# A two-block network on one core: bias products behind the fourth unit, and modulation rows on four column tiles

## The chip, the cores and the metric

One core of one Trainium2 chip runs one program, in float32. The metric is the device time of an execution in microseconds; lower is better.

## The reference

The reference computes two blocks on a sequence of 512 tokens of width 1024. The first has an input projection, native sparse attention with a bias by distance, a convolution branch, gated linear attention (GLA), a gated FFN and a per-layer embedding gate (PLE). The second has a modulated norm over 512 tokens and 256 context tokens, a Fourier branch, an RWKV branch and a convolutional FFN. Two parts of it matter here. One is the bias row of the attention, a table of 32 buckets by 8 heads read by distance and masked:

```python
def head_bias(dist):
    return bias_h[:, t5_bucket(dist)].reshape(Hk, G, *dist.shape)
```

The other is the modulation: six vectors of 1024 for the tokens (`c`) and six for the context (`c_ctx`), 6144 numbers each:

```python
mod_x = jax.nn.silu(c) @ ada_w[l] + ada_b[l]
sh1, sc1, g1, sh2, sc2, g2 = [m[:, None, :] for m in jnp.split(mod_x, 6, axis=-1)]
h = modulate(rms_norm_2(x, norm1_g[l]), sh1, sc1)
```

The weights of the modulation, 1024 x 6144, do not depend on the first block, so their products can be done anywhere before the second.

## The kernel before, in words

All arrays lie in one SBUF tensor and are transposed: 128 channels on the partitions, tokens in the free dimension. Weights come as **units** of 128 x 8 x 128 floats (512 KB), in one fixed order (`STREAM`), through a ring of four slots. SyncE loads the ring (L2368, L2372): four units at the start, then unit n + 4 into the slot of unit n as soon as TensorE's products on unit n are done (`units_done`). In the common use of a unit (`product`, L331) eight products of 128x128 by 512 columns are summed in a PSUM bank; one takes two matmul records in the trace.

Each engine runs its own list, stage by stage, and semaphores tie them. The order on each engine is written out by hand.

**Start** (`start`, then `norm1`). ScalarE's queue issues four tiles of x, the constants (identity and ones), the columns of small parameters, and three small arrays for the bias (`onehot`, `rel_bias`, `negmask`). All five arrays after x count on one semaphore, `ld_start`. TensorE waits for all five, multiplies the bias table with the one-hot array (L450, two products of 8 x 320), and then sums the squares of `norm1` with a matrix of ones (L399). ScalarE makes the squares (L369), then the logarithm and exponential of the root (L373, L374), VectorE scales the tiles (L407), and the 17 units of the input projection follow (`project1`, L331). VectorE adds the mask to the bias row (L461), and ScalarE later stores it to DRAM and reads it back as tiles.

**Modulation rows** (`ada_units`, L905). The weights are 48 units, four for each of twelve blocks `b` of 512 columns. Of unit q of a block, two products have the pair of activated vectors (`cs`, two columns) as weights and 512 columns of the unit as the moving operand; eight such products are summed in a bank of 2 x 512. ScalarE copies the two rows to `modrow` (`ada_row`, L921). When six blocks are there, 24 small transposes bring each piece of 2 x 128 to 128 x 2 (`ada_turn`, L915), and VectorE adds the bias column (`ada_columns`, L926).

Where these units stand:

- blocks 0 to 5 in the GLA stage: four units first, with the sum of the context's squares behind them (L895); one unit in each of the eight chunks of the recurrence, between the product with the state (L1021) and the update of the state (L1027, which VectorE's L1063 and L1064 follow); then four units, a sum of squares (L1034), eight units, the turn;
- block 6 behind the sum of the norm ahead of the first FFN, block 7 behind that of the norm ahead of the PLE gate: they cover the time in which ScalarE and VectorE make the root and the first scaled tile;
- block 8 ahead of the sum of the last norm of the first block (L393, L395), which waits for POOL's additions (L385);
- blocks 9 to 11 right behind that sum, then the sum of the second block's norm (L399) and the second turn.

For the steps of the prediction: L735 are transposes of 128x128 in the attention, L672 the narrow products of the compression MLP (weights 128x64, two column tiles), L1812 the wide products of the RWKV recurrence (64x64 tiles, 128 columns, four positions in turn), L1053 VectorE's multiply that makes the scaled key of the GLA, L961 the exponential it needs.

## Time and profile before

| | us |
|---|---|
| median of 3 runs | 2170.36 (2165.15 to 2174.89) |
| profiled execution, its own time | 2162.62 |
| profiled execution, span of the trace | 2160.4 |
| TensorE matmul busy | 2006.7 (93%) |
| VectorE busy | 759.6 (35%) |
| ScalarE busy | 483.2 (22%) |
| POOL busy | 193.7 (9%) |
| mean granted TensorE clock | 0.958 of full |

The span is from the first to the last instruction. Busy times of engines overlap. The weight loads of TensorE are listed by themselves (PEld) and run beside its matmuls. In 2160 us the DMA engines move 157.73 MB, 73 GB/s on the mean.

### The profile page before, as it was taken

The numbers are of one execution on the slowest core, as the hardware profiler recorded it, in microseconds if no ns is written. First come the engines' busy times: TensorE is split into PE (matmuls) and PEld (weight loads), VectorE is DVE, ScalarE is ACT, GpSimd is POOL, SyncE is SP. The second block draws the span as 40 slices with busy tenths as digits, with TensorE's granted clock in tenths as the row PEclk, the third lists the DMA queues.
The fourth block names the chain that finished last, engine by engine and source line by source line (L and its number), as shares of the span: only waits on it lengthen the run. The fifth ranks groups of instructions, "written<-read, shape, count | busy, mean of one in ns | idle before, by whom it ended". The sixth has DMA issues, their size and how long they took to land.

```text
span 2160.4 us, 33132 instructions
## 1 busy us (share of the span) xinstructions
PE 2006.7 (93%) x13434; PEld 1052.2 (49%) x13434; DVE 759.6 (35%) x1508; ACT 483.2 (22%) x992; POOL 193.7 (9%) x274
## 2 busy tenths in 40 slices
PE   6996898899999999999899995898989899999997
PEld 2444775243444444444245543888864344444443
DVE  1702243201000000002122245666642588888101
ACT  1101265201000000001321224344441322221001
POOL 0000010010000000000100001645421000000000
PEclk9997599999999999999999996999999999999999
DMA  3621001523222222223531100000011222222222
GB/s 110 237 68 49 1 1 64 175 84 102 78 77 71 75 87 78 88 87 98 175 146 52 59 20 16 4 5 5 4 47 58 62 75 78 78 78 78 71 84 97
DMA packets 43847, 157.73 MB, mean 73 GB/s; under 512 B 5016, under 2 KB 5672, under 8 KB 42840
## 3 DMA queue, kind: packets, MB, share of 16 engines
q1 hardware_dynamic: 37440, 133.19, 19.6%
q10 hardware_dynamic: 6296, 22.90, 2.9%
q8 instruction: 90, 1.47, 0.3%
q14 instruction: 21, 0.17, 0.0%
HBM read 151.32 MB, written 6.31 MB: 73 GB/s over the span
## 4 chain that ended last, share of the span: by engine, by line
PE 73%; DVE 5%; ACT 2%; issue 1%; POOL 1%; DMA 0%; ACTq 0%; DVEq 0%; POOLq 0%
PE psum L331 38%; PE psum L1101 19%; PE psum L905 4%; PE psum L1738 2%; PE psum L1742 2%; PE psum L1523 1%; DVE mem L1897 1%; DVE mem L1925 1%; PE psum L1197 1%; PE psum L1749 1%; DVE mem L1924 1%; PE psum L1770 1%; PE psum L1566 0%; ACT mem L2033 0%; PE psum L1836 0%
## 5 line engine op out<-in xcount | busy, mean ns | idle before, releaser
L331 PE MATMUL psum<-mem 128*128 128x512 f32 (+1 forms) x2272 | 949.7, 580 | 11.1 <-ACT mem L380 7.2
L331 PEld LDWEIGHTS psum<-mem 128*128 128x128 f32 x2272 | 431.0, 190 | 528.1 <-issue 516.1
L1101 PE MATMUL psum<-mem 128*128 128x512 f32 x960 | 414.2, 592 | 4.3 <-DVE mem L2217 2.6
L1101 PEld LDWEIGHTS psum<-mem 128*128 128x128 f32 x960 | 181.1, 189 | 236.4 <-issue 228.7
L2298 DVE SCALAR_TENSOR_TENSOR mem<-mem 128x512 f32<-128x512 f32 x352 | 235.1, 747 | 0.0
L385 POOL TENSOR_TENSOR mem<-mem 128x512 f32<-128x512 f32 x30 | 38.0, 1267 | 1183.5 <-ACT mem L369 1183.1
L369 ACT ACTIVATE mem<-mem 128x512 f32<-128x512 f32 x56 | 33.7, 625 | 394.3 <-DVE mem L1114 200.2
L1172 DVE TENSOR_TENSOR mem<-mem,psum 128x512 f32 x22 | 15.2, 690 | 287.3 <-PE psum L331 287.3
L905 PE MATMUL psum<-mem 128*2 128x512 f32 x192 | 87.4, 606 | 0.0
L1738 PE MATMUL psum<-mem 64*64 64x64 f32 x1920 | 74.9, 222 | 12.0 <-DVE mem L1925 4.1
L1114 DVE TENSOR_TENSOR mem<-mem,psum 128x512 f32 x16 | 11.0, 688 | 211.5 <-PE psum L1101 211.5
L1742 PE MATMUL psum<-mem 64*64 64x64 f32 x1920 | 73.4, 222 | 3.1 <-issue 2.9
L1116 DVE SCALAR_TENSOR_TENSOR mem<-psum,mem 128x512 f32 x16 | 12.0, 751 | 177.6 <-PE psum L1101 177.6
L1738 PEld LDWEIGHTS psum<-mem 64*64 64x64 f32 x1920 | 65.4, 136 | 18.0 <-DVE mem L1925 9.8
L1742 PEld LDWEIGHTS psum<-mem 64*64 64x64 f32 x1920 | 65.7, 136 | 5.9 <-issue 3.9
L1997 ACT COPY mem<-psum 128x256 f32<-128x256 f32 x120 | 45.1, 376 | 89.4 <-PE psum L1738 87.9
L2267 ACT COPY mem<-psum 128x512 f32<-128x512 f32 x44 | 25.9, 588 | 174.5 <-PE psum L331 174.3
L407 DVE SCALAR_TENSOR_TENSOR mem<-mem 128x512 f32<-128x512 f32 x56 | 37.7, 746 | 65.7 <-ACT mem L374 65.7
L1924 DVE COPY_PREDICATED mem<-mem,psum 128x256 f32<-128x256 int32 x96 | 41.1, 429 | 33.4 <-PE psum L1742 33.3
L905 PEld LDWEIGHTS psum<-mem 128*2 128x2 f32 x192 | 15.2, 85 | 64.9 <-issue 59.5
L790 DVE CUSTOM_DVE_ANT_0 mem<-psum,mem 128x128 f32<-128x128 f32 (+3 forms) x64 | 28.9, 490 | 50.7 <-PE psum L722 50.7
L665 PE MATMUL psum<-mem 128*128 128x62 f32 x128 | 27.5, 421 | 20.6 <-DVE mem L649 20.6
(291 smaller groups left out, 1771.6 us busy)
## 6 DMA issues: line engine op xcount, KB each, us to landing
mem<-in_units SPq DMA_DIRECT2D x248, 512.0 KB, 3.6
mem<-in_cw ACTq DMA_DIRECT2D x2, 2048.0 KB, 17.4
mem<-in_wn ACTq DMA_DIRECT2D x1, 2144.0 KB, 9.4
bias_tiles<-bias_scratch ACTq DMA_DIRECT2D x1, 2048.0 KB
mem<-bias_tiles ACTq DMA_DIRECT2D x1, 2048.0 KB, 9.5
x_scratch<-mem ACTq DMA_DIRECT2D x1, 2048.0 KB, 8.5
mem<-in_dft ACTq DMA_DIRECT2D x1, 2048.0 KB, 14.1
mem<-x_scratch ACTq DMA_DIRECT2D x1, 2048.0 KB, 8.0
```

The lines of the kernel that those rows point to most:

```text
L331: last = pe.matmul(dst, ring[:, slot, k, :], rhs(k), start=(k == 0), stop=(k == 7))
L369: eng.activation(sqr[:, k, 0:n], src(k), ACT.Square).then_inc(squared, 1)
L385: steps.link(eng.tensor_tensor(sqr[:, 0, 0:n], sqr[:, 0, 0:n], sqr[:, k, 0:n], ALU.add))
L407: eng.scalar_tensor_tensor(dst(k), src(k), g(k), rstd[:, 0:n], ALU.mult, ALU.mult).then_inc(scaled, 1)
L790: last = eng.tensor_tensor_reduce(sc[u % 2][g][:, 0:n], bank[:, 0:n], bias[:, h, 128 * (3 - i):512], -1.0, 1e20, ALU.add, ALU.min, low[u % ...
L905: last = eng.matmul(ps[ada_bank(b)][0:2, :], cs[:, 2 * q + k:16:8], ring[:, slot, 4 * k:4 * k + 4, :].rearrange("p a b -> p (a b)"), start ...
L1101: last = eng.matmul(ps[m % 4], ring[:, slot, k - 8 * part, :], rhs(k), start=(k == 0), stop=(k == ktiles - 1))
L1738: each(lambda hp, c, t: eng.matmul(dst(E_[d], hp, t), g[t, hp, 1, :], T[t, hp, :], start=True, stop=True)).then_inc(q["made"], 1)
L1742: each(lambda hp, c, t: eng.matmul(dst(O_[d], hp, t), a[t, hp, :], b_[t, hp, :], start=True, stop=True)).then_inc(q["made"], 1)
L1924: steps.link(eng.copy_predicated(split(T), bc22(kept), heads(O_[d])))
L1997: eng.copy(split(s["Z"]), heads(E_[d])).then_inc(q["kept"], 1)
L2298: steps.did_but(1, lambda: eng.scalar_tensor_tensor(cacc[:, j], src, w, cacc[:, j], ALU.mult, ALU.add))
```

## The change

The bias products leave the start: TensorE waits there for the constants alone, which have a semaphore of their own and are issued between the x tiles, and the two bias products stand behind the fourth unit of the input projection, in banks 4 and 5. SyncE waits for x tiles 5 and 6 before it loads the ring. The pair of activated vectors becomes 32 columns wide, 30 of them zero. A modulation product covers 128 columns of a unit instead of 512, and four of them go to four column tiles, so that the result stands on all 128 partitions (four strips of 32) and 128 columns. Copies and `modrow` have that shape, and six transposes of 128x128 in two banks turn six blocks. The squares of the context get a place of their own.

```diff
-LOADS = {"start": 5, "compress": 4, "gla": 3, "fourier": 2, "low_rank": 2, "rwkv": 4}
+LOADS = {"start": 4, "compress": 4, "gla": 3, "fourier": 2, "low_rank": 2, "rwkv": 4}
...
-        modrow = r_ada.take(12, 512)
-        sqc = modrow[:, 0:4, :].rearrange("p a b -> p (a b)").rearrange("p (k t) -> p k t", k=KT)
-        cs = r_ada.take(16)
+        sqc = r_ada.take(KT, CTX)
+        modrow = r_ada.take(12, P)
+        cs = r_ada.take(8, 32)
...
-                for k in range(1, KT, 2):
+                for k in (1, 3):
                     eng.dma_start(xT[:, k, :], A["xT"][:, k, :]).then_inc(x_in[k], 16)
-                load(eng, "start", mem[:, ident.offset:ident.offset + 3 * P], A["consts"])
+                load(eng, "consts", mem[:, ident.offset:ident.offset + 3 * P], A["consts"])
+                for k in (5, 7):
+                    eng.dma_start(xT[:, k, :], A["xT"][:, k, :]).then_inc(x_in[k], 16)
...
             def sp(eng, steps):
                 for k in range(0, KT, 2):
                     eng.dma_start(xT[:, k, :], A["xT"][:, k, :]).then_inc(x_in[k], 16)
+                eng.wait_ge(x_in[5], 16)
+                eng.wait_ge(x_in[6], 16)
 
             def pe(eng, steps):
-                arrived(eng, "start")
-                for n in range(2):
-                    last = eng.matmul(ps[1 + n][0:8, 0:320], relb[0:32, :], onehot[0:32, 320 * n:320 * n + 320],
-                                      start=True, stop=True)
-                last.then_inc(biased, 1)
+                arrived(eng, "consts")
...
             def pe(eng, steps):
-                linear_pe(eng, u0, 17, lambda k: hT[:, k, 0:S], free, ready=ready)
+                def unit(m):
+                    def f(slot, j, i):
+                        eng.wait_ge(free, m + 1)
+                        return product(eng, slot, lambda k: hT[:, k, 0:S], ps[m % 4], ready)
+                    return f
+
+                for m in range(17):
+                    per_unit(eng, u0 + m, 1, unit(m))
+                    if m == 3:
+                        arrived(eng, "start")
+                        for n in range(2):
+                            last = eng.matmul(ps[4 + n][0:8, 0:320], relb[0:32, :], onehot[0:32, 320 * n:320 * n + 320],
+                                              start=True, stop=True)
+                        last.then_inc(biased, 1)
...
             def dve(eng, steps):
+                eng.wait_ge(biased, 1)
+                for n in range(2):
+                    steps.did(eng.tensor_tensor(bvec[0:8, 320 * n:320 * n + 320], ps[4 + n][0:8, 0:320],
+                                                negmask[0:8, 320 * n:320 * n + 320], ALU.add))
+                steps.wait()
+                eng.sem_inc(bias_put, 1)
                 conv_taps(eng, steps)
...
             def pool(eng, steps):
+                eng.memset(cs, 0.0)
...
-            eng.activation(cs, col("c", 0, 16), ACT.Silu).then_inc(cond, 1)
+            eng.activation(cs[:, :, 0:2], view(col("c"), 0, [[1, 8], [8, 2]]), ACT.Silu).then_inc(cond, 1)
...
                 for k in range(2):
-                    last = eng.matmul(ps[ada_bank(b)][0:2, :], cs[:, 2 * q + k:16:8],
-                                      ring[:, slot, 4 * k:4 * k + 4, :].rearrange("p a b -> p (a b)"),
-                                      start=(q == 0 and k == 0), stop=(q == 3 and k == 1))
+                    for c in range(4):
+                        last = eng.matmul(ps[ada_bank(b)][32 * c:32 * c + 32, 0:P], cs[:, 2 * q + k, :],
+                                          ring[:, slot, 4 * k + c, :], start=(q == 0 and k == 0), stop=(q == 3 and k == 1))
...
-            for t in range(4 * first, 4 * last_ + 4):
-                last = eng.transpose(ps[bank][:, 2 * t:2 * t + 2], modrow[0:2, t // 4, P * (t % 4):P * (t % 4) + P],
-                                     ident[0:2, 0:2])
+            for b in range(first, last_ + 1):
+                n = b - first
+                last = eng.transpose(ps[bank + n // 4][:, P * (n % 4):P * (n % 4) + P], modrow[:, b, :], ident)
...
-            eng.copy(modrow[0:2, b, :], ps[ada_bank(b)][0:2, :]).then_inc(got, 1)
+            eng.copy(modrow[:, b, :], ps[ada_bank(b)][:, 0:P]).then_inc(got, 1)
...
-            steps.link(eng.tensor_tensor(mod[:, lo:hi, :], ps[bank][:, 2 * lo:2 * hi].rearrange("p (t v) -> p t v", v=2),
-                                         view(col("ada_b", lo), 0, [[1, hi - lo], [0, 2]]), ALU.add))
+            for n, at in enumerate(range(lo, hi, 16)):
+                to = min(at + 16, hi)
+                steps.did(eng.tensor_tensor(mod[:, at:to, :].rearrange("p (b c) v -> p b c v", c=4),
+                                            view(ps[bank + n], 0, [[P, (to - at) // 4], [32, 4], [1, 2]]),
+                                            view(col("ada_b", at), 0, [[4, (to - at) // 4], [1, 4], [0, 2]]), ALU.add))
+            steps.wait()
```

The order of TensorE's instructions at the start, before, with the semaphores that each row waits for (a row is a run of equal instructions, its size that of the result):

```order
L450 MATMUL psum<-mem 8x320 [waits ld_start]
L450 MATMUL psum<-mem 8x320
L399 MATMUL psum<-mem 128x512 [waits norm_squared] x8
L321 UNCONDITIONAL_BRANCH
L321 ISA
L338 ISA [waits landed0]
L331 MATMUL psum<-mem 128x512 [waits norm_scaled,in1_free]
L331 MATMUL psum<-mem 128x512 [waits norm_scaled] x7
```

And now (L554 are the bias products):

```order
L399 MATMUL psum<-mem 128x512 [waits norm_squared,ld_consts]
L399 MATMUL psum<-mem 128x512 [waits norm_squared] x7
L331 MATMUL psum<-mem 128x512 [waits norm_scaled,in1_free,landed0]
L331 MATMUL psum<-mem 128x512 [waits norm_scaled] x7
L331 MATMUL psum<-mem 128x512 [waits norm_scaled,in1_free,landed1]
L331 MATMUL psum<-mem 128x512 [waits norm_scaled] x7
L331 MATMUL psum<-mem 128x512 [waits norm_scaled,in1_free,landed2]
L331 MATMUL psum<-mem 128x512 [waits norm_scaled] x7
L331 MATMUL psum<-mem 128x512 [waits norm_scaled,in1_free,landed3]
L331 MATMUL psum<-mem 128x512 [waits norm_scaled] x7
L554 MATMUL psum<-mem 8x320 [waits ld_start]
L554 MATMUL psum<-mem 8x320
```

The norm's sum comes first and waits for the constants and the squares; the wait for the small loads stands behind four units. The hardware loop over groups of four units is gone from this stage.

TensorE's order in the last chunk of the GLA recurrence and behind it, before:

```order
L1021 MATMUL psum<-mem 64x64 x4
L905 MATMUL psum<-mem 2x512 x2
L1027 MATMUL psum<-mem 32x64 x4
L905 MATMUL psum<-mem 2x512 x8
L1034 MATMUL psum<-mem 128x512 x2
L905 MATMUL psum<-mem 2x512 x16
L915 MATMUL psum<-mem 128x2 x24
```

And now (L1037, L918, L1043, L1050 and L928 are the lines 1021, 905, 1027, 1034 and 915 of before):

```order
L1037 MATMUL psum<-mem 64x64 x4
L918 MATMUL psum<-mem 32x128 x8
L1043 MATMUL psum<-mem 32x64 x4
L918 MATMUL psum<-mem 32x128 x32
L1050 MATMUL psum<-mem 128x512 x2
L918 MATMUL psum<-mem 32x128 x64
L928 MATMUL psum<-mem 128x128 x6
```

Nothing changes its place here. A unit is eight products instead of two, and the turn six instead of 24.

## Rows read from the trace of the kernel before

**Rows 1.** The page: busy time of TensorE, its share and its matmul records.

```profile
PE 2006.7 (93%) x13434; PEld 1052.2 (49%) x13434; DVE 759.6 (35%) x1508; ACT 483.2 (22%) x992; POOL 193.7 (9%) x274
```

**Rows 2.** The page, costliest groups: busy us, mean ns of one, idle before.

```profile
L905 PE MATMUL psum<-mem 128*2 128x512 f32 x192 | 87.4, 606 | 0.0
```

**Rows 3.** Timeline of 0 to 31 us: start us, us, engine line op.

```profile
2.64 0.58 ACTq L304 DMA_DIRECT2D mem<-in_consts  x1
...
7.15 4.25 ACT L369 ACTIVATE mem<-mem 128x512 f32<-128x512 f32 x8
15.54 2.30 PE L450 MATMUL psum<-mem 32*8 32x320 f32 x4 [15.54 <-DMA mem<-in_negmask]
...
17.77 8.77 PE L399 MATMUL psum<-mem 128*128 128x512 f32 x16
...
26.57 0.69 ACT L373 ACTIVATE mem<-psum,mem 128x512 f32<-128x512 f32 x1 [15.17 <-PE psum L399]
```

**Rows 4.** Timeline of 17 to 26 us, weight loads alone.

```profile
20.49 0.34 PEld L399 LDWEIGHTS psum<-mem 128*128 128x128 f32 x1 [0.52 <-issue]
...
21.64 0.19 PEld L399 LDWEIGHTS psum<-mem 128*128 128x128 f32 x1 [0.24 <-issue]
```

**Rows 5.** Groups by form on TensorE, and one row of the timeline of its weight loads.

```profile
L735 PE MATMUL psum<-mem 128*128 128x128 f32 x168 | 29.9, 311 | 7.0 <-ACT mem L840 4.8 <-ACT mem L844 1.8
...
L672 PE MATMUL psum<-mem 128*64 128x31 f32 x8 | 0.6, 298 | 1.2 <-ACT mem L638 1.2
...
1434.70 0.91 PEld L1812 LDWEIGHTS psum<-mem 64*64 64x64 f32 x32
```

**Rows 6.** Timeline of the head of the GLA stage.

```profile
375.55 0.61 ACT L961 ACTIVATE mem<-mem 128x512 f32<-128x512 f32 x1
...
379.14 0.69 DVE L1053 TENSOR_TENSOR mem<-mem 128x512 f32<-128x512 f32 x1
```

**Rows 7.** Timeline of one chunk of the GLA loop.

```profile
401.09 0.09 PEld L905 LDWEIGHTS psum<-mem 128*2 128x2 f32 x2
402.90 0.15 PEld L1027 LDWEIGHTS psum<-mem 64*32 64x32 f32 x8 [0.86 <-issue]
...
404.12 0.09 PEld L905 LDWEIGHTS psum<-mem 128*2 128x2 f32 x2
```

**Rows 8.** DMA: landing of in_units, and busy time, clock, DMA share, GB/s of 9 to 12 us.

```profile
DMA to landing us min/median/max: 3.3/3.6/12.1
...
9.00:12.00 3.00, 0.00 (x0) 0.00 (x0) 0.00 (x0) 2.40 (x5) 0.00 (x0) 1.00 1.02 400
```

**Rows 9.** Windows with small products: us, busy times (instructions), PEclk, DMA share, GB/s.

```profile
250.00:265.00 15.00, 15.00 (x76) 12.02 (x76) 5.92 (x35) 6.53 (x27) 1.82 (x4) 0.50 0.01 2
383.00:386.00 3.00, 3.00 (x69) 2.32 (x68) 0.00 (x0) 0.62 (x2) 0.00 (x0) 0.50 0.03 5
```

**Rows 10.** Timeline behind the chunk loop, to the turn of the rows.

```profile
409.22 7.03 PE L905 MATMUL psum<-mem 128*2 128x512 f32 x16
...
418.09 14.00 PE L905 MATMUL psum<-mem 128*2 128x512 f32 x32
...
432.13 0.57 ACT L921 COPY mem<-psum 2x512 f32<-2x512 f32 x1 [6.40 <-PE psum L905]
432.76 1.67 PE L915 MATMUL psum<-mem 2*128 2x2 f32 x24 [0.67 <-ACT mem L921]
```

**Rows 11.** Timeline of the norm ahead of the first FFN.

```profile
493.32 7.03 PE L905 MATMUL psum<-mem 128*2 128x512 f32 x16
...
496.19 5.39 DVE L407 SCALAR_TENSOR_TENSOR mem<-mem 128x512 f32<-128x512 f32 x8 [4.64 <-ACT mem L374]
```

**Rows 12.** Timeline of the end of the first block.

```profile
1044.58 1.64 PE L393 MATMUL psum<-mem 128*128 128x512 f32 x2 [3.39 <-POOLq L386]
...
1047.86 21.05 PE L905 MATMUL psum<-mem 128*2 128x512 f32 x48
...
1068.84 7.15 PE L399 MATMUL psum<-mem 128*128 128x512 f32 x16
```

More of the change, by code:

```diff
@@ L249, in build @@
         gl_o = r_gl.take(2, S)
[L251 removed]
+        r_ada = Region(SB_COLS - 2 * KT * CTX - 2 * CTX - 12 * P - 8 * 32, SB_COLS)
         assert r_gl.at <= r_ada.at
[L253 to L255 removed]
+        sqc = r_ada.take(KT, CTX)
+        modrow = r_ada.take(12, P)
+        cs = r_ada.take(8, 32)
         ctxT = r_ada.take(KT, CTX)
@@ L457, in dve @@
                 eng.sem_inc(sem("eps_set"), 1)
-                arrived(eng, "start")
-                eng.wait_ge(biased, 1)
-                for n in range(2):
-                    steps.did(eng.tensor_tensor(bvec[0:8, 320 * n:320 * n + 320], ps[1 + n][0:8, 0:320],
-                                                negmask[0:8, 320 * n:320 * n + 320], ALU.add))
-                steps.wait()
-                eng.sem_inc(bias_put, 1)
                 arrived(eng, "start")
@@ L545, in project1 @@
             free, nat = sem("in1_free"), sem("in1_nat")
+            biased, bias_put = sem("biased"), sem("bias_put")
             nat_copied, gates_read = sem("in1_nat_copied"), sem("in1_gates_read")
```

2 lines of the change are left out of this document (removed).

## The prediction

> **What bounds the kernel now.** I read the page first, then the timeline around each place that the change touches, then the groups by form, the DMA landings and the granted clock. The page says that TensorE is busy for 93% of the span [rows 1], so only time taken off TensorE's own stream, or off a wait in front of it, counts. The modulation products (line 905) are 192 matmul records, 87.4 us, with no idle time before them [rows 2]. Each product of the program is two records, so this is 48 units of four records, 1.82 us each with the ends that overlap. They occupy the array for a result of two rows.
>
> The start is the second place. The eight squares begin at 7.15 us, but TensorE does nothing before 15.54 us, when the last small load (negmask) lands. The bias products then take 2.2 us, the norm sum 8.77 us, and ScalarE's logarithm follows at 26.57 [rows 3]. The constants that the sum needs were issued at 2.64 us, long before. The first records of the sum follow each other at 0.86 us (0.34 busy and 0.52 idle for the weight load), later ones at 0.43 us [rows 4]: TensorE begins at its lower level, 1.2 GHz, and reaches 2.4 GHz about 5.7 us after its first work.
>
> **Start.** The sum now waits for the constants alone, which are issued ahead of two x tiles, and for the squares. I let it begin when the first square is done, at 7.8. If the rise again comes 5.7 us after the first work, seven records run at 0.86 and nine at 0.43: 6.0 + 3.9 us and a tail of 0.1, end near 17.8 instead of 26.5, a gain of 8.8 us. All sixteen at 0.86 would leave 5.0; the old duration of 8.77 would give 10.0. The four records of the bias products come back behind the fourth unit: 320 of 512 columns at 0.43 is 0.27 each, 1.1 us, and 0.1 for the change of tile size; their old 2.2 us is the other end. VectorE's two additions there are beside the next unit, and the store of the bias row is not due until ScalarE has issued its other loads. The ring's first four loads now wait for x tiles 5 and 6; they have until about 21 us, while 2 MB at the 400 GB/s of this start takes 5.2 us [rows 8]. I price that wait at nothing; if the x tiles came only at 15 us it would begin to show. Net **7.6 us**, between 2.8 and 8.9.
>
> **One unit.** Instead of two products of 512 columns there are eight of 128 columns, on four column tiles: sixteen records. If one tile had to end before the next began, each record would last its 128 columns, 0.43 / 4 = 0.107 us, and a unit 1.72 us, as now. The nearest row with four tiles at work is line 1812: its 32 weight loads, one per record of 128 columns on 64x64 tiles, take 0.91 us [rows 5], 28 ns a record where 107 would be serial. So four tiles do run together, two neighbouring records of one tile included. Sixteen records are then 0.45 us; I take 0.5. The far end is 1.72 and beyond (rivals).
>
> The Trainium skill ("TensorE: Matmul & The Clock Gate", Part 3) says that matmuls start and end strictly in program order. Taken literally for this order (both records of a tile, then the next tile) each second record would hold up the next tile and a unit would take 0.86 us, 2.9 us less gain over the eight units of the chunk loop; by that rule the row of line 1812 could not show 28 ns, so the trace does not bear it out.
>
> **Head of the GLA stage.** The first four units end earlier, but the context sum behind them waits for ScalarE's squares, and VectorE's multiply (line 1053, at 379.14) needs an exponential that ends at 376.16 [rows 6]. Between nothing and 3.0 us; I take **1**, since TensorE is at its lower level there and idles where it was filled before.
>
> **Chunk loop.** The period of a chunk is 3.03 us (401.09 to 404.12), and 1.81 of it lie between the unit's first product and line 1027 [rows 7]. The rest is the recurrence with VectorE, which stays. At 2.4 GHz the 1.81 become 0.54: 1.27 us less, eight times, 10.2. At 1.2 GHz the unit takes 0.9 and the small products about 0.4 longer: 0.48 less, 3.8 in all. The clock is the open point. In 250 to 265 us TensorE has work all the time, small products, and is granted 0.50; after the small tiles at 380 us it falls to 0.50 for 383 to 386 [rows 9]. The new loop does less array work per us than the old. I take **7**, between the two ends.
>
> **Twelve units behind the loop.** From 409.22 to the last row copy at 432.13 there are 22.9 us [rows 10]. TensorE would need only 12 x 0.5 plus two products of line 1034, so the ring sets the pace: the last of the first four was issued when the loop's last unit was used, and lands 3.6 us later (the median landing) [rows 8]; eight more follow at no less than 524 KB / 400 GB/s = 1.31 us each. 3.6 + 10.5 + 0.5 = 14.6 us at best, a gain of 8.3; with ScalarE's squares and line 1034 in between I take **7.5**. The other end is 6.
>
> **Turning the rows.** The copy reads 128 instead of 512 columns (0.57 us, about 0.3 less). The 24 small transposes take 1.67 us [rows 10]; six of 128x128 at 29.9 us / 168 records = 0.18 [rows 5] take 1.1. VectorE has one more operation, 0.25. **0.6 us** once; the second turn is beside the root of the norm. What follows a stretch in which TensorE waits for loads is likely to begin at 1.2 GHz: four to eight records of the next stage at 0.86 instead of 0.43, and line 1034 as well. I charge **2.5 us** (0 to 4.3).
>
> **Norms of the first FFN and of the PLE stage.** Four units cover the norm's chain and last 7.03 us from 493.32; VectorE's first scaled tile is there at 496.19 + 0.7 [rows 11]. With the units at 0.5 us the products behind wait for the slot that the first unit frees: 493.8 + 3.6 = 497.4. Gain 2.9, less 0.8 for a chance of the lower clock: 2.1, and the same pattern in the PLE norm: **4.2** for both (2.4 to 5.8).
>
> **End of the first block.** Unit group 8 gives nothing: TensorE then already idles 3.39 us for POOL's additions [rows 12], and only idles longer. Groups 9 to 11 are 21.0 us (1047.86 to 1068.84). Four units are in the ring; the first refill, issued after 0.9 us at the lower clock, lands at 4.5, seven more at 1.31, and 0.5: 14.2. Gain 6.8, less 2.4 for line 399 at half clock behind it: **4.4** (3.4 to 6.8).
>
> **Sum.** 7.6 + 1 + 7 + 7.5 + 0.6 - 2.5 + 4.2 + 4.4 = 29.8 us. The profiled execution took 2162.6 us (2160.4 of span, 2.2 around it), so 2132.8 of its kind; it was a short one, and the median of the runs is 2170.4. From that: **2140 us**.
>
> **Rivals.** *Full clock everywhere* (chance 0.15): no charge for the clock, 7.6 + 2 + 10.2 + 7.5 + 0.6 + 5.8 + 6.8 = 40.5, 2130 us. For it: in the loop before, TensorE kept its clock with gaps in every chunk. Against: rows 9.
>
> *Low clock* (0.14): loop 3.8, tail 6.5, turn 0.3, charge 3.4, norms 2.4, end 3.4, head 0, start 7.6: 20.6 gained, 2150 us. The rows for it are 383 to 386 and 250 to 265 [rows 9]. The Trainium skill speaks for this rival ("TensorE: Matmul & The Clock Gate", the section on HAM oscillation): short bursts with waits for DMA between them start cold every time.
>
> *The tiles do not run together* (0.09): with 128 rows each, four streams cross all partitions, which no row with 128 columns shows. Records then take 107 ns, units stay as they are, and only the start, turn and copies are left: about 8.4 us, 2162 us.
>
> *Slower* (0.04): serial tiles whose weight loads stay exposed. Line 672, the only one with 128 rows on narrower column tiles, needs 0.6 / 8 = 75 ns a record where 31 columns last 26 [rows 5]: 49 ns exposed. Then 107 + 49 = 156 ns, 2.5 us a unit, 0.75 us more on 44 units (group 8 is hidden) is +33, less 8.4: +25 us, 2195 us. It decides from 1.72 + 8.4 / 44 = 1.91 us a unit, 119 ns a record. Against it: line 1812.
>
> **Numbers.** Forecast 2140 us with 0.57; 2130 with 0.15, 2150 with 0.14, 2162 with 0.09, 2195 with 0.04, and 0.01 for the rest. The range of 2124 to 2158 takes in the first three with the bounds of the start and of the tail and some 5 us between runs; it leaves out the last two and the ends. About 0.5% (11 us) is what a measurement of this kernel can tell from no change: faster than 2159.5 is 0.87, with the forecast and both clock cases; the serial case and a little of the low-clock one are within, 0.09; slower 0.04.
>
> **What would show it.** Right: the sum's first record near 8 us and the logarithm near 18; two bias products between the fourth and fifth unit; a dense unit of 16 records in 0.45 to 0.6 us; a chunk period of 1.8 to 2.6 us; line 918 waiting for in_units in the two long groups, with 1.3 to 1.5 us from unit to unit; the products behind the FFN norm waiting for a ring slot at about 4 us after the sum. Wrong: units of 1.7 us (the tiles do not overlap), a granted clock of 1.00 (then 2130) or of 0.50 all through the GLA stage (then 2150), or constants that land later than the squares.

## The result and the profile after

| | before | after |
|---|---|---|
| median of 4 runs, us | 2170.95 (2165.15 to 2174.89) | 2140.82 (2137.85 to 2151.81) |
| profiled execution, its own time | 2162.62 | 2138.96 |
| its span | 2160.4 | 2136.7 |
| mean granted clock | 0.958 | 0.944 |

The ratio is 0.9878, with a 95% interval of 0.984 to 0.9916: the change makes the kernel 1.2% faster, clear of the noise, and the time is the predicted one to a microsecond. The profiled executions differ by less, 23.7 us, and a later batch of runs gave 0.9913 (0.9896 to 0.9929). Both are taken up below.

The two lines of the page that answer to [rows 1] and [rows 2] (busy us and records; then mean ns of one, and idle before):

```profile
PE 1964.6 (92%) x13974; PEld 1063.3 (50%) x13974; DVE 759.9 (36%) x1510; ACT 479.4 (22%) x992; POOL 194.0 (9%) x275
...
L918 PE MATMUL psum<-mem 128*32 128x128 f32 x768 | 37.4, 347 | 16.3 <-DMA mem<-in_units 16.3
```

The modulation products are four times as many records and cost 37.4 us instead of 87.4. So 50 us went off TensorE's work there, and 16.3 us came back as waits for units. TensorE's whole busy time fell by 42.1 us only, as other work ran more at half clock (mean granted clock 0.944 for 0.958). That is the first reading. The second is the span cut at the same events in both profiled executions (starts of TensorE's records; "norm sum" is the last product of the sum, on L395):

| stretch, us | before | after | gained |
|---|---|---|---|
| start of the span to the GLA stage (bias products in both) | 363.68 | 354.12 | 9.56 |
| head: GLA stage to its first chunk | 21.37 | 20.00 | 1.37 |
| eight chunks | 24.17 | 18.13 | 6.04 |
| behind the chunks, to the output projection | 26.17 | 22.79 | 3.38 |
| output projection, to the norm sum | 56.87 | 59.44 | -2.57 |
| norm sum to the products of the first FFN | 8.20 | 5.37 | 2.83 |
| first FFN | 470.33 | 470.31 | 0.02 |
| norm sum to the products of the PLE gate | 8.20 | 5.26 | 2.94 |
| PLE gate, to the last norm sum | 67.03 | 69.15 | -2.12 |
| twelve units, to L399 | 22.82 | 19.18 | 3.64 |
| L399 and the norm, to the second block's input | 11.50 | 13.74 | -2.24 |
| the rest of the span | 1080.06 | 1079.21 | 0.85 |

**Start.** Timeline of 0 to 51 us, the rows that answer to [rows 3, 4]:

```profile
1.68 0.46 ACTq L304 DMA_DIRECT2D mem<-in_consts  x1
...
6.93 4.26 ACT L369 ACTIVATE mem<-mem 128x512 f32<-128x512 f32 x8
...
7.76 8.55 PE L399 MATMUL psum<-mem 128*128 128x512 f32 x16 [7.76 <-DMA mem<-in_consts]
...
9.63 0.33 PEld L399 LDWEIGHTS psum<-mem 128*128 128x128 f32 x1 [0.52 <-issue]
...
10.99 0.19 PEld L399 LDWEIGHTS psum<-mem 128*128 128x128 f32 x1 [0.24 <-issue]
...
16.36 0.69 ACT L373 ACTIVATE mem<-psum,mem 128x512 f32<-128x512 f32 x1 [5.17 <-PE psum L399]
...
49.36 1.24 PE L554 MATMUL psum<-mem 32*8 32x320 f32 x4
```

The sum starts with the constants at 7.76, and the logarithm follows at 16.36 instead of 26.57. The first records follow each other at 0.86 us, and from 10.99 us on at 0.43: the clock rose 3.1 us after TensorE's first work, where before it was 5.7. This differs between executions. In the other profiles with the new start four to seven records run at 0.86 us, where this one has three, the sum lasts 8.8 to 10.0 us (here 8.6), and the logarithm comes between 16.54 and 18.09 us. The bias products cost 1.2 us at their new place, at 49.36.

**Chunk loop.** Timeline, weight loads alone; each row begins one chunk (answers to [rows 7]). Then three windows: us, busy times (instructions) of PE, PEld, DVE, ACT and POOL, PEclk, DMA share, GB/s.

```profile
374.12 0.30 PEld L1037 LDWEIGHTS psum<-mem 32*64 32x64 f32 x8
...
376.68 0.21 PEld L1037 LDWEIGHTS psum<-mem 32*64 32x64 f32 x8 [0.93 <-DVE mem L1080]
...
378.48 0.21 PEld L1037 LDWEIGHTS psum<-mem 32*64 32x64 f32 x8 [0.80 <-DVE mem L1080]
...
380.41 0.30 PEld L1037 LDWEIGHTS psum<-mem 32*64 32x64 f32 x8 [0.88 <-DVE mem L1080]
...
382.91 0.30 PEld L1037 LDWEIGHTS psum<-mem 32*64 32x64 f32 x8 [0.88 <-DVE mem L1080]
```

```profile
372.00:376.00 4.00, 3.99 (x96) 3.10 (x96) 0.00 (x0) 0.90 (x2) 0.00 (x0) 0.57 0.01 4
376.00:380.00 4.00, 2.45 (x64) 1.52 (x64) 1.12 (x5) 0.00 (x0) 0.00 (x0) 0.91 0.66 224
380.00:392.00 12.00, 9.04 (x158) 5.41 (x160) 2.24 (x10) 0.27 (x1) 0.00 (x0) 0.50 0.71 223
```

A chunk takes 1.80 us at full clock (376.68 to 378.48) and 2.50 at half clock (380.41 to 382.91). The first takes 2.56 us, with the clock still low (0.57 in the window at 372). Two begin at full clock; from 380 us on the granted clock is 0.50 and stays there, so six of the eight chunks lie at the low clock.

**Behind the chunks.** Timeline (answers to [rows 10]), then windows with the columns as above:

```profile
396.66 1.08 PE L918 MATMUL psum<-mem 128*32 128x128 f32 x16 [1.62 <-DMA mem<-in_units]
...
397.67 3.00 PE L1050 MATMUL psum<-mem 128*128 128x512 f32 x4
...
404.74 0.64 PE L918 MATMUL psum<-mem 128*32 128x128 f32 x16 [1.70 <-DMA mem<-in_units]
...
408.44 1.08 PE L918 MATMUL psum<-mem 128*32 128x128 f32 x16 [3.06 <-DMA mem<-in_units]
...
409.70 1.08 PE L918 MATMUL psum<-mem 128*32 128x128 f32 x16 [0.19 <-DMA mem<-in_units]
...
412.43 1.54 PE L928 MATMUL psum<-mem 128*128 128x128 f32 x6 [0.39 <-ACT mem L933]
```

```profile
400.00:412.00 12.00, 6.61 (x130) 3.77 (x128) 4.46 (x5) 3.75 (x6) 0.00 (x0) 0.77 0.80 287
415.00:419.00 4.00, 3.96 (x5) 1.83 (x6) 0.00 (x0) 0.00 (x0) 0.00 (x0) 0.50 0.26 103
```

From unit to unit it can be 1.26 us (408.44 to 409.70), 524 KB / 1.26 us = 416 GB/s, but others follow after 2.4 and 3.7 us, and the mean over the stretch is 287 GB/s. TensorE is busy half of the time, and what follows begins at half clock (the window at 415). Line 1050 has a part in this. It takes 3.0 us (397.67 to 400.61), and while TensorE is on it no slot comes free: between 395.3 and 401.4 us SyncE issues one load. The next four, issued from 401.45 to 403.57, land at 404.69, 408.39, 409.66 and 410.92.

**Norms and the end of the block.** The four units at the PLE norm, the products behind the norms (answers to [rows 11]), and the last group (answers to [rows 12]):

```profile
479.85 2.38 PE L331 MATMUL psum<-mem 128*128 128x512 f32 x5 [2.37 <-DVE mem L407]
...
951.22 1.95 PE L918 MATMUL psum<-mem 128*32 128x128 f32 x64
...
955.42 2.21 PE L331 MATMUL psum<-mem 128*128 128x512 f32 x3 [2.25 <-DMA mem<-in_units]
...
1030.95 0.65 PE L918 MATMUL psum<-mem 128*32 128x128 f32 x16 [1.93 <-DMA mem<-in_units]
...
1033.57 0.65 PE L918 MATMUL psum<-mem 128*32 128x128 f32 x16 [1.97 <-DMA mem<-in_units]
...
1042.74 1.08 PE L918 MATMUL psum<-mem 128*32 128x128 f32 x16 [1.21 <-DMA mem<-in_units]
...
1043.75 9.38 PE L399 MATMUL psum<-mem 128*128 128x512 f32 x16
```

Four units together take 1.95 us at full clock, which is 30 ns a record. The products behind the norms wait 2.3 us where the units used to stand. The last sum takes 9.38 us and not 7.15: it begins at half clock. In the last group the first refill is used 4.5 us after the group's first product (1026.42 to 1030.95), and the seven after it are spread over 11.8 us. Their loads land 4.2 to 6.4 us after their issue, while the page's median for all loads of units is 3.3.

### The profile page after: what moved, and what is told of

Its sections match the earlier page's. It is cut to its first block, busy times and chain, and to the rows that moved or that the text cites. A ratio compares the mean times of both kernels' runs of the same rounds, so it can differ in the third digit from the quotient of the medians.

```text
span 2136.7 us, 34186 instructions
## 1 busy us (share of the span) xinstructions
PE 1964.6 (92%) x13974; PEld 1063.3 (50%) x13974; DVE 759.9 (36%) x1510; ACT 479.4 (22%) x992; POOL 194.0 (9%) x275
## 4 chain that ended last, share of the span: by engine, by line
PE 71%; DVE 5%; ACT 3%; DMA 1%; issue 1%; POOL 1%; ACTq 0%; DVEq 0%; SPq 0%; POOLq 0%
PE psum L331 38%; PE psum L1117 19%; PE psum L1754 2%; PE psum L1758 2%; PE psum L1539 1%; DVE mem L1913 1%; DMA mem<-in_units 1%; PE psum L918 1%; PE psum L1213 1%; PE psum L1765 1%; DVE mem L1941 1%; PE psum L1786 1%; DVE mem L1940 1%; ACT mem L2049 1%; PE psum L1582 1%
## 5 line engine op out<-in xcount | busy, mean ns | idle before, releaser
L1754 PE MATMUL psum<-mem 64*64 64x64 f32 x1920 | 74.3, 222 | 12.5 <-DVE mem L1941 5.3
L1754 PEld LDWEIGHTS psum<-mem 64*64 64x64 f32 x1920 | 64.7, 136 | 19.0 <-DVE mem L1941 11.8
L918 PE MATMUL psum<-mem 128*32 128x128 f32 x768 | 37.4, 347 | 16.3 <-DMA mem<-in_units 16.3
L676 PE MATMUL psum<-mem 128*128 128x62 f32 x128 | 27.5, 421 | 21.2 <-DVE mem L660 21.2
L765 PE MATMUL psum<-mem 128*128 128x65 f32 x320 | 42.6, 283 | 3.3 <-ACT mem L868 3.3
## 6 DMA issues: line engine op xcount, KB each, us to landing
mem<-in_cw ACTq DMA_DIRECT2D x2, 2048.0 KB, 17.3
mem<-in_dft ACTq DMA_DIRECT2D x1, 2048.0 KB, 14.2
```

What stands on the lines that cost most here:

```text
L765: last = eng.matmul(bank[:, at:at + 65], pt[u % 2][g][:, kb * P:(kb + 1) * P], vx[:, kb, 2 * b + g, 0:65], start=(kb == 0), stop=(kb == i))
L918: last = eng.matmul(ps[ada_bank(b)][32 * c:32 * c + 32, 0:P], cs[:, 2 * q + k, :], ring[:, slot, 4 * k + c, :], start=(q == 0 and k == 0), ...
L1754: each(lambda hp, c, t: eng.matmul(dst(E_[d], hp, t), g[t, hp, 1, :], T[t, hp, :], start=True, stop=True)).then_inc(q["made"], 1)
```

## The experiments

Ratios are to the kernel before on the same chip. Experiments 1, 2, 4 and 7 shared one chip; 3, the half units of 5, 6 and 8 ran on a second, the eighths of 5 on a third. For the first measurement the chip is not on record. Runs with a single time serve for their traces.

**1 and 2: each part alone.** The modulation as before, with the new start; and the new modulation with the old start.

```diff
# 1, in ada_units, cut (copies, turn and modrow as before too)
-                    for c in range(4):
-                        last = eng.matmul(ps[ada_bank(b)][32 * c:32 * c + 32, 0:P], cs[:, 2 * q + k, :],
+                    last = eng.matmul(ps[ada_bank(b)][0:2, :], cs[:, 2 * q + k:16:8],
# 2, at the start, cut (against the changed kernel)
-                arrived(eng, "consts")
+                arrived(eng, "start")
+                for n in range(2):
+                    last = eng.matmul(ps[1 + n][0:8, 0:320], relb[0:32, :], onehot[0:32, 320 * n:320 * n + 320],
```

> The kernel before with the new start alone (bias products behind the fourth unit, constants on their own semaphore, ring loads held for x tiles 5 and 6); modulation as before. My reading of the trace after the change: the logarithm of the first norm at about 16.4 us instead of 26.6, the bias products 1.2 us later in the stream, and nothing given back later, so 9 us less than before (ratio 0.996). Rival: part of it is lost again, because ScalarE's stall on the store of the bias row and the wait for the small loads of the GLA stage do not move with TensorE; then under 5 us.

> The changed kernel with the start and the input projection of before: modulation on four column tiles alone. If the parts add up, the rest of the gain: 14 us less than before (ratio 0.9935). The chunk period is 1.8 us where TensorE is granted its full clock and 2.5 us where it is not. Rival (the parts help each other, or the start moved the clock's fall): 18 us or more, or 10 or less.

Measured: 1 gives 2159.24 us, ratio 0.9981 (0.9963 to 0.9998); 2 gives 2151.03, ratio 0.9941 (0.992 to 0.9961). The logarithm is at 16.54 us in 1 and at 27.95 in 2. In 1 the products of the second block's Fourier branch begin 9.84 us earlier than before, but the stretch behind them, in which no code is changed, was 6.1 us longer in its profiled execution (363.3 for 357.2). The medians add to a ratio of 0.992, the traces to 9.8 + 17.7 us (1266.75 against 1249.04). The start is worth nearly 10 us and the tiles 18 at that milestone, and neither needs the other. They do not quite add up: both together gain 24.0 us there (25.8 in the repetition of experiment 8), not 27.5. The difference is within what stretches without any edit vary by: the attention alone took 152.2 us in 2 and 154.7 in the changed kernel.

For 2 the expected 14 us came (13.6 by the medians). For 1 they did not: 5.4 us by the medians, ratio 0.9981 for 0.996, near the rival's "under 5". The rival's reason is not what the trace shows, for the GLA stage begins 9.6 us earlier (354.09 for 363.68). What took the gain back in the profiled execution is the stretch of the second block, and why it was longer stays open.

**3: the order of the tiles.** In the change both records of a product go to one tile and then the next tile follows; here the two products of a tile stand together.

```diff
-                for k in range(2):
-                    for c in range(4):
+                for c in range(4):
+                    for k in range(2):
```

> The changed kernel with the two loops inside a unit exchanged: the two products of one column tile follow each other, so four records in a row use the same tile; the result is the same. If matmul records start strictly in order and a tile must be free for its next record, four records in a row hold up the next tile, and a dense group of four units (1.95 us at full clock in the trace after the change) takes 4 us or more. If tiles have queues of their own, it stays within 0.3 us of 1.95.

One time, 2144.99 us. Timeline, the four units at the first FFN's norm:

```profile
474.70 2.02 PE L918 MATMUL psum<-mem 128*32 128x128 f32 x64
```

2.02 us where the changed kernel has 1.95, not 4. Four neighbouring records on one tile cost practically what two cost. The starts of the single records in the two traces say how. They come in waves of four, the waves 109 ns apart (133 for the first), which is the time of 128 columns at full clock. Inside a wave the starts are 6 to 7 ns apart in the changed kernel and mostly 13 to 15 ns here, where twice as many records stand between one tile and the next. I read this as records handed out in program order, some 3 ns each, each tile keeping its later ones behind its own first; the trace does not name the tile of a record, so this is an inference.

**4: the clock in the chunk loop.** One product more in each chunk, which nobody reads; it stands where TensorE waits for VectorE.

```diff
+                    if n >= 4:
+                        eng.wait_ge(got, 4)
+                    eng.matmul(ps[2 + n // 4][:, 0:384], ident, hT[:, 0, 0:384], start=True, stop=True)
```

> The changed kernel with one product more per chunk of the GLA recurrence, 384 columns into a bank that nobody reads, behind the update of the state, where TensorE waits about 0.9 us for VectorE. It computes nothing that is used. If the lower clock comes from too little work in the array, the clock stays at 1.00 in the loop, the period falls from 2.5 to 1.8 us, and the loop from 18.1 to about 15 us in spite of the added work: 3 to 4 us less than the changed kernel. If the clock has another cause, the period is 2.5 us or more (the product takes 1.3 us at half clock and no longer fits the wait): up to 3 us more.

Timeline of two chunks and the window of 380 to 387 us (columns as above):

```profile
380.73 0.91 PE L1048 MATMUL psum<-mem 128*128 128x384 f32 x2
...
382.66 0.91 PE L1048 MATMUL psum<-mem 128*128 128x384 f32 x2
```

```profile
380.00:387.00 7.00, 7.00 (x128) 3.84 (x128) 1.73 (x8) 0.57 (x2) 0.00 (x0) 1.00 0.82 270
```

The chunk takes 1.93 us instead of 2.50, though it does more, and the clock is 1.00. The loop is 14.7 us, for 18.1. Of the difference 1.4 us are not the product's doing, since this loop already began at full clock. Five other profiles without the product did that too and took 16.6 to 17.0 us, so it gives about 2 us. The clock is the cause: in all eight profiles of column tiles without it the chunk goes to 2.5 us after two to four at 1.8 to 2.2 us, and in all four with it no chunk behind the first is over 1.94. So the low clock was the price, and useless work removes it. Its size and kind were not varied. The whole time does not show it: 2144.84 us, ratio 0.9889 (0.9852 to 0.9925), because the stretch of the Fourier and RWKV branches was 365.2 us in the profiled execution, for 356.5. Experiment 8 repeats the question with more rounds.

**5: what the ring costs.** Only the first half, then only the first eighth of each unit is loaded, from the fifth unit on; TensorE's work is the same. Left out is therefore that part of all weights.

```diff
-                    eng.dma_start(ring[:, j], units[4 * i + j]).then_inc(landed[j], 16)
+                    eng.dma_start(ring[:, j, 0:4], units[4 * i + j][:, 0:4]).then_inc(landed[j], 16)
```

> The changed kernel in which SyncE's loop loads only the first half of every unit (256 KB instead of 512), so all products from the fifth unit on use stale data in their second half; products and waits are the same. Question: what paces the long groups of modulation units, 19.9 us (twelve behind the chunk loop, to the last row copy) and 17.3 us (twelve at the end of the first block). If it is the bytes of the ring, the groups fall to what TensorE and the latency of one load allow: (3.0 + 0.9) / 4, about 1.0 us a unit, so about 12 and 12 us. If it is a fixed cost of each load (issue, wait, landing), they stay near 19 and 17.

> The changed kernel with only the first eighth of each unit loaded into the ring from the fifth unit on (64 KB of 512); TensorE's work is unchanged and reads what stands in the slot. So the outputs are left without seven eighths of the weights. With half of each unit the last group of twelve units took 14.4 us where the whole ones take 19.2, which is 4.8 us for the 2.1 MB that its eight loads then lack, 440 GB/s. Theory (bytes at that rate on top of a fixed part, made of the landing time of about 3.3 us of the first refill and of TensorE's own 0.5 to 1.1 us a unit): 19.2 - 7/8 x 9.5 = 10.8 us for the group, and the eight units behind the loop come down alike. Rival (the loads' own round trips through the four slots set a floor, however small they are): the group stays above 13 us, with waits for in_units of 1 us or more still in front of single units.

| us | whole | half | eighth |
|---|---|---|---|
| twelve units at the end of the block | 19.18 | 14.41 | 11.69 |
| behind the chunks, to the output projection | 22.79 | 15.66 | 14.06 |
| time of the one run | 2138.96 | 2134.47 | 2129.42 |

Timeline of the version with eighths, two rows of the last group:

```profile
1018.52 0.64 PE L918 MATMUL psum<-mem 128*32 128x128 f32 x16 [1.16 <-DMA mem<-in_units]
...
1024.51 0.65 PE L918 MATMUL psum<-mem 128*32 128x128 f32 x16 [1.09 <-DMA mem<-in_units]
```

Bytes set most of the pace: the first half of them is worth 4.8 us in the last group, and 7.5 us of 19.2 go with seven eighths. The last group with whole units took 19.2 to 21.8 us in seven profiles, so one execution of each version is enough to show the direction, though not the tenths. The half-unit version does what was expected: 14.4 us less 1.8 for the sum's last product is 12.6 for the twelve units (about 12 expected). The rest is not quite the straight line expected (11.7, not 10.8). The median time from issue to landing is 3.3 us with 512 KB, 2.7 with 256 and 1.9 with 64, and single waits of a microsecond remain with loads of 64 KB, so a part of the gaps comes from the round trip through the slots. The floor of 13 us that the rival set is not there.

**6: the wait of the ring at the start.** SyncE issues the first four units at once.

```diff
-                eng.wait_ge(x_in[5], 16)
-                eng.wait_ge(x_in[6], 16)
```

> The changed kernel without SyncE's wait for x tiles 5 and 6: the ring's first four loads are issued at once, beside those of x. I priced that wait at nothing. If the loads share the bandwidth, the small loads and the constants land later, the sum of the first norm begins later than 7.8 us and the first logarithm comes after 16.4, by up to 5 us; then the wait is part of the gain. If not, both stay within 0.5 us.

One time, 2148.06 us. The sum of the norm begins at 7.78 us, and between 7.60 and 8.15 in the other profiles with the new start, all of them with the wait. So the constants do not land later without it. The logarithm is at 17.65, and between 16.36 and 18.09 in the others; this spread is that of the clock's rise. The wait is no part of the gain at the start. The GLA stage began at 360.0 us in this run, later than in any other with the same stages ahead of it (352.6 to 357.3); whether that has to do with the wait cannot be told from one run.

**7: other places for the units.** 24 of them in the attention stage, where the DMA queues are nearly empty (2 GB/s at 250 us [rows 9]), eight in the chunks, and no group longer than four.

```diff
-STREAM = [("in1", 17), ("ada", 24), ("out1", 8), ("ada6", 4), ...
+STREAM = [("in1", 17), ("ada", 36), ("out1", 8), ("ada9", 4), ...
...
-                    eng.wait_ge(exped, u + 1)
                     if u:
                         eng.wait_ge(kept, u)
+                    if u < 24 and u % 4 == 3:
+                        ada_units(eng, u - 3, 4)
+                    eng.wait_ge(exped, u + 1)
```

> The changed kernel with other places for the units, the same products: blocks 0 to 5 in six bursts of four units in the attention stage (ahead of a wait for ScalarE's exponentials), block 6 at the head of the GLA stage, 7 and 8 in its chunks, 9 and 10 behind the two norms, 11 where TensorE waits for POOL. So no long group is left in which TensorE waits for the ring. If the long groups (19.9 us and 17.3 us in the trace after the change) are bound by the ring's loads, they go, line 1050 and its squares stay (about 6 us), and the attention grows by six bursts of 1.8 us at full clock or 3.6 at half: 10 to 20 us less than the changed kernel. If the groups were bound by TensorE's own products at half clock, the bursts cost as much in the attention and the gain is under 5 us.

2136.17 us (2126.86 to 2141.71), ratio 0.9864 (0.9827 to 0.9901). The long groups are gone: the last norm sum to L399 takes 6.14 us for 19.18, the stretch behind the chunks about 14 for 22.8. But the attention is 14.1 us longer (168.8 for 154.7): 24 units there cost 0.59 each, and they cover nothing. This price is rough, because the attention without any unit took 151.6 to 159.2 us in ten profiles. The changed kernel did not run on this chip. Against its two ratios, 0.9878 and 0.9913, the places alone give 3 to 11 us; the 10 to 20 expected are not shown, and the smaller value cannot be told from none.

**8: places and unused products together.** 16 units in the attention, and unused products in the chunks, behind the first sum, behind the units of the norms and behind the turns.

```diff
+        def fill(eng, bank, times=1):
+            for _ in range(times):
+                eng.matmul(ps[bank][:, 0:3 * P], ident, mem[:, ident.offset:ident.offset + 3 * P], start=True, stop=True)
...
+                    if u < 16 and u % 4 == 3:
+                        ada_units(eng, u - 3, 4)
```

> The version with other places, improved: blocks 0 to 3 in four bursts in the attention, 4 at the head of the GLA stage, 5 and 6 in its chunks, 7 ahead of the sum of squares and 8 behind it (both beside the chain of ScalarE and VectorE that bounded the tail of the spread version), 9 to 11 as in the spread version. And filler products of 384 columns that nobody reads, where TensorE waits anyway: one per chunk, and 3 to 5 behind the sums of the norms, so that the clock stays up. Against the spread version: attention 5 us less, chunk loop 3 us less, 1.5 to 2 us less behind each of four norms; 12 to 15 us less in all, 18 to 22 less than the changed kernel (ratio to before about 0.978). If the clock at the start of a stage does not hang on the wait ahead of it, only the first 8 come.

2110.6 us (2107.02 to 2125.97, 6 runs), ratio 0.9756 (0.9719 to 0.9794). It beats both kernels. Its runs fall into two groups, four of 2107.0 to 2112.4 us and two of 2125.9 and 2126.0. The last batch, on one chip, takes it apart: the unused products alone with the places of the change, the changed kernel again, and this version again.

```diff
# unused products alone; fill as above
+                        after_sum=lambda eng: fill(eng, 6, 5))
...
+                    fill(eng, 2 + n // 4)
...
-                        after_sum=lambda eng: ada_units(eng, 24, 4), late_rows=lambda eng: ada_row(eng, 6))
+                        after_sum=lambda eng: (ada_units(eng, 24, 4), fill(eng, 6, 3)), late_rows=lambda eng: ada_row(eng, 6))
```

> The changed kernel with its units where they are, and with unused products alone: five of 384 columns behind the first norm's sum, one in each of the eight chunks, three behind the units at the feed-forward norms and at the per-layer norm, four behind the second turn. Theory (array work of small size lets the granted clock fall, and the long products behind it then run at half clock): granted clock near 1.00 in the chunk loop, loop about 3 to 3.5 us shorter than in the changed kernel (18.1 us), the stretch from the first logarithm's products to the comparison about 2 us shorter, the stretch from the per-layer norm to the next sum 67.4 us and not 69.2, the stretch from the second block's input to its fourth milestone about 3 us shorter; in all 8 to 11 us under the changed kernel, a ratio to the kernel before of about 0.983. Rival (the gain of the version with both came from the places of the units alone): under 3 us, a ratio of about 0.987. The two long groups of units stay as they are in both.

> The changed kernel once more, on the same chip as the other two, as their common base: a ratio to the kernel before of about 0.988, its loop at 18 us, its last group of units at 19 us.

> Units spread and unused products, once more, on the same chip: a ratio of about 0.976, which is some 26 us under the changed kernel of the same chip if the places and the products add up (places about 12 us by the shorter groups less the attention's growth, products 8 to 11); if most of it was luck of the stage that no edit touches, 15 us or less.

| | median, us | ratio, 95% |
|---|---|---|
| the changed kernel again | 2147.62 (2146.12 to 2150.05) | 0.9913 (0.9896 to 0.9929) |
| unused products alone | 2135.58 (2133.26 to 2139.22) | 0.9859 (0.9842 to 0.9875) |
| places and unused products | 2117.0 (2115.26 to 2118.02) | 0.9765 (0.9749 to 0.9781) |

Window of the chunk loop with the unused products alone (columns as above); the changed kernel has 0.50 there:

```profile
380.00:387.00 7.00, 7.00 (x128) 3.68 (x126) 1.73 (x8) 0.27 (x1) 0.00 (x0) 1.00 0.78 249
```

With the unused products the median is 12 us lower, and all four runs are below all four of the changed kernel. The two profiled executions differ by 12.9 us of span. By place:

| place, us | changed kernel again | unused products alone | gained | elsewhere |
|---|---|---|---|---|
| eight chunks | 16.7 | 14.8 | 1.8 | without them 16.6 to 18.1, with them at most 15.3 |
| behind the first sum, to the attention | 179.0 | 177.5 | 1.6 | without them 178.1 to 180.5, with them 177.5 |
| second block's input to its Fourier branch | 185.1 | 181.9 | 3.2 | without them 184.9 to 185.3, with them 181.9 |
| PLE gate | 69.1 | 67.4 | 1.7 | 67.4 in three versions without them too |
| the two norms | 11.0 | 12.7 | -1.8 | the products stand in the way |

The first three rows hold in every profile (the second by 0.6 us at least), so they are shown to be theirs: 6.6 us, less 1.8 at the norms, about 5. The PLE gate's 1.7 is not shown, because the half units, the eighths and experiment 7 have the short gate without any unused product. Another 2 us lie in the last group (21.5 to 19.5), less 0.9 behind it, and small stretches, 8.9 in the Fourier and RWKV stage, and 4.4 are lost in the attention, all with the same code. So more than half of the 12 us is not traced to the unused products.

With the units in other places as well, the median falls by another 18.6 us, 15.1 in the profiled executions: 13.4 in the last group (19.54 to 6.15), 5.8 behind the chunks (21.1 to 15.3), 2.7 in the output projection and 1.6 at the PLE norm, less 8.7 by which the attention grows (159.2 to 167.9). That last price is uncertain: in the first profile of this version the attention with its 16 units took 159.4.

**Why one batch showed 30 us and another 19.** Between the two batches the median of the kernel before went down by 4.1 us (2170.95 to 2166.9), and that of the changed kernel up by 6.8 (2140.82 to 2147.62). The second has a place in the trace. Lines of one group, the wide products of the second block, in the changed kernel's first profile and in its repetition:

```profile
L1582 PE MATMUL psum<-mem 64*128 64x512 f32 x32 | 21.3, 814 | 4.3 <-DVE mem L1553 3.3 <-DVE mem L1549 0.9
```

```profile
L1582 PE MATMUL psum<-mem 64*128 64x512 f32 x32 | 27.3, 1010 | 4.8 <-DVE mem L1553 3.9 <-DVE mem L1549 0.9
```

The same 32 records cost 21 us in ten of the fourteen profiled executions of this study and 27.3 in the four others (the repetition, experiment 4 and both of 5): 1010 ns a record for 814. No version edits this stage. It is most of the 8.9 us above. Up to the Fourier branch the repetition is even 1.8 us ahead of the first profile (1240.99 for 1242.77); from there to the second block's output projection it loses 8.5. What decides in which execution the clock is low there is open: the three profiles with unused products behind the second turn all have 21 us, but so do seven without them.

## Why the prediction was right, and where not

By its own terms, in us gained (the profiled executions, rows of the table above):

| term | predicted | measured |
|---|---|---|
| start, with the bias products | 7.6 | 9.6 |
| head of the GLA stage | 1 | 1.4 |
| chunk loop | 7 | 6.0 |
| twelve units behind the loop and the turn | 8.1 | 3.4 |
| half clock behind it | -2.5 | -2.6 |
| two norms | 4.2 | 3.7 |
| end of the first block | 4.4 | 1.4 |
| the rest | 0 | 0.9 |
| sum | 29.8 | 23.7 |

- **The unit** was right: 0.5 us taken, 0.49 measured (1.95 / 4), at full clock. The four tiles run together, and 1.72 us, the serial case, is excluded. The Trainium skill ("TensorE: Matmul & The Clock Gate", Part 3) says that matmuls start and end strictly in program order. Together with the prediction's own assumption that a tile must be free for its next record, this would have given 0.86 us. The trace does not bear the two out together: a new tile starts every 6 to 7 ns, though both records of the tile before stand ahead of it. Experiment 3 shows that their order hardly matters.
- **Start**: the mechanism was right, and 2 us more came than forecast. 1.4 of them are the sum, which lasted 8.6 us and not 10, because the granted clock rose 3.1 us after the first work and not 5.7. That was this execution: in others the sum took up to 10.0 and the logarithm came at up to 18.09, as forecast. The sum began with the constants (7.76), 0.3 us behind the first square, so the sign "constants that land later than the squares" was there, too small to matter. The wait of the ring was priced at nothing; experiment 6 does not contradict that.
- **Chunk loop**: right in size, between the two clocks as taken. 1.80 and 2.50 us a chunk were inside the predicted 1.8 to 2.6. The choice of 7 was a middle between two ends, not a mechanism, and that six of eight chunks would run at the low clock was not foreseen; in the repetition, where fewer did, 7.5 us were gained. Experiment 4 shows the clock as the cause. Full clock everywhere held nowhere, the low-clock rival in most chunks. The Trainium skill's section on HAM oscillation (same page) speaks of bursts between DMA waits that start cold every time. The trace agrees behind the longest wait: the unit at 408.44, after 3.06 us, takes 1.08 us, and the clock is 0.50 at 415. It does not agree for every burst: the units at 404.74, 1030.95 and 1033.57, after 1.7 to 2.0 us, take 0.64 or 0.65, full clock. In the chunk loop the clock fell at gaps for VectorE.
- **The two long groups** failed as sizes: together 12.5 us predicted (8.1 + 4.4), 4.8 measured. The step was "eight more follow at no less than 524 KB / 400 GB/s = 1.31 us each", with one landing of 3.6 us in front. It was called the best case; then 0.8 us were taken off in the one group and nothing in the other. Measured are 1.26 us between some units and 2.3 to 3.7 between others, 287 GB/s on the mean, so the sign of 1.3 to 1.5 us from unit to unit did not come. In the last group the first refill came after 4.5 us, as forecast; the seven behind it took 11.8 us for 9.2, and the last unit 1.0 for 0.5. Half clock in the sum behind it cost 2.24 us, for 2.4 predicted, so the group's own length, 17.3 us for 14.2, made the miss. In the first group the prediction let line 1034 (now L1050) run beside the loads; it took 3.0 us at half clock and held up the slots. Experiment 5 shows that bytes are most of the pace. Why loads in flight together are spread so unevenly stays open. The last group itself varies, 19.2 us in the first profile and up to 21.8 in others with the same code there: with the sum behind it, its gain lies between -1.5 and 1.6 us in seven profiles (1.4 in the first).
- **Norms**: 2.8 and 2.9 us gained as worked out (2.9 each), less 2.1 in the PLE gate behind one of them (granted clock 0.76 from 955 to 962 us), for a charge of 1.6 in all. The first waited for VectorE's tile, not for the slot that the prediction named; the second for the slot.
- **The total**: the hit to a microsecond is luck. The sum was 6 us too high against the profiled execution (2132.8 forecast, 2138.96 measured), and the median hit, 2140.8, because the medians lie 30.1 us apart where the two profiled executions lie 23.7 apart. The prediction named the short execution of before and counted from the median, which helped it. The low-clock rival, 2150 us, is nearer to the repetition's 2147.6; both lie in the range, and its chance of 0.14 was low.

## What to carry to other kernels

A matmul whose weights have few columns can be split over column tiles: here sixteen records of 128 columns cost 0.49 us where four of 512 cost 1.82. What follows must be asked twice: the loads that the slow products had paced become the wait (price it by the mean rate of the ring over a whole group, not by its best spacing), and the engine with less to do can lose its clock. Then check whether a few unused products in its idle slots give more than they cost; here the median with them was 12 us lower (about 5 of them shown in the places where they stand), and with units in short groups another 18.6.

## What was not expected of the hardware

- Products that nobody reads shortened a chunk from 2.50 to 1.93 us, with the granted clock at 1.00 for 0.50.
- The ring gave 287 GB/s over a group of units, though 416 GB/s between some of them and 400 at the start [rows 8]. With several loads in flight each landed 4.2 to 6.4 us after its issue, for a median of 3.3.
- A unit's records start in waves of four, one on each tile by my reading, every 109 ns at full clock.
- The clock's rise and fall move from run to run where nothing is edited: three to seven slow records in the first sum, 21 or 27.3 us for the same 32 records. The same attention stage took 151.6 to 159.2 us. A difference of 6 to 10 us between versions needs the trace as well as the median.
